# Moving 25 small weight strips out of a state scan, and a gate product made of seven smaller ones

## The reference, cut to what matters

```python
sh_a, sc_a, g_a, sh_f, sc_f, g_f = split(silu_c @ w_mod + b_mod, 6)      # "modulation", 6 x 1024 columns
hx = x * (1 + sc_a) + sh_a                                               # the first two sixths are needed early
proj = hx @ w_in                                                         # z, q, xbc, dt, k, v
y = ssd_scan(forward) + ssd_scan(backward) + xs * d_skip                 # chunked state scan, 8 chunks of 128 tokens
y = y * silu(z);  y = y * rsqrt(mean(y*y over each half)) * ssd_norm_g   # the gate, z = hx @ w_in[:, 0:1024]
q, k = rope(rms_norm(q)), rope(rms_norm(k))
o = softmax(q @ [k_ctx, k].T) @ [v_ctx, v]
x = layer_norm(alpha * x + g_a * ([y, o] @ w_out))                       # g_a and later ones: the second modulation
```

## Time and profile before

| | us |
|---|---|
| median of 3 runs | 3060.01 |
| profiled execution, its own time | 3059.18 |
| span of its trace | 3057.1 |
| PE busy in the span | 2879.1 (94%) |
| DVE, ACT, POOL busy | 1593.1, 749.8, 1078.1 |
| granted TensorE clock, mean | 0.969 |

### The profile page before, as it was taken

One profiled execution on the slowest core, in us unless ns is written; L12 is line 12 of the kernel. 1 busy time (PEld: TensorE's weight loads), 2 busy tenths in 40 slices (PEclk: granted clock), 3 DMA queues, 4 the chain that ended last, 5 costly groups with the idle time before them and its releaser, 6 DMA issues. The chain is left out here.

```text
span 3057.1 us, 28739 instructions
## 1 busy us (share of the span) xinstructions
PE 2879.1 (94%) x10163; PEld 1404.6 (46%) x10163; DVE 1593.1 (52%) x2480; ACT 749.8 (25%) x1573; POOL 1078.1 (35%) x971
## 2 busy tenths in 40 slices
PE   7998999999899999999869994988999999999999
PEld 4554554444444444344534442565444444444443
DVE  2434884345767777556654435455644444444446
ACT  2223755511133333400311115222030000000002
POOL 0001881000177777700022004831024555555442
PEclk9999999999899999999879996999999999999999
DMA  7001332100100000020368987003020111111101
GB/s 279 21 0 31 95 103 73 55 28 1 56 1 1 1 1 1 1 70 24 89 249 347 375 318 239 4 14 111 1 83 28 42 55 62 49 42 42 42 14 62
DMA packets 130686, 237.51 MB, mean 78 GB/s; under 512 B 25544, under 2 KB 81520, under 8 KB 120688
## 3 DMA queue, kind: packets, MB, share of 16 engines
q1 hardware_dynamic: 120016, 206.11, 19.0%
q0 software_dynamic: 5760, 16.78, 1.8%
q10 hardware_dynamic: 4768, 12.79, 1.1%
HBM read 235.65 MB, written 26.22 MB: 86 GB/s over the span
## 5 line engine op out<-in xcount | busy, mean ns | idle before, releaser
L3614 DVE TENSOR_TENSOR arena_d<-arena_d,ps 128x512 f32<-128x512 f32 x154 | 102.0, 686 | 387.6 <-PE ps L3489 387.6
L3454 POOL TENSOR_TENSOR arena_b<-arena_b,arena_d 128x512 f32<-128x512 f32 x120 | 150.9, 1271 | 362.6 <-DVE arena_d L3636 361.3
L1383 DVE TENSOR_REDUCE arena_b<-ps 128x1 f32<-128x512 f32 (+1 forms) x384 | 212.0, 597 | 122.8 <-PE ps L1263 119.9
L1365 POOL TENSOR_TENSOR arena_b<-arena_b 128x512 f32<-128x512 f32 x182 | 224.8, 1272 | 70.8 <-ACT arena_b L1346 70.8
L3633 DVE TENSOR_TENSOR arena_b<-arena_b,ps 128x512 f32<-128x512 f32 x240 | 158.9, 685 | 32.5 <-POOL arena_b L3454 23.7
L1263 PE MATMUL ps<-arena_d,arena_a 64*128 64x512 f32 (+1 forms) x768 | 169.7, 529 | 3.0 <-DVE arena_b L1374 2.9
L1281 PE MATMUL ps<-arena_a,arena_d 64*128 64x512 f32 x640 | 169.3, 600 | 0.0
L1077 PE MATMUL ps<-ring,arena_b 128*128 128x512 f32 x384 | 167.4, 592 | 0.0
L564 PE MATMUL ps<-arena_b,ring 128*128 128x512 f32 x384 | 167.1, 593 | 0.0
L3489 PE MATMUL ps<-arena_a,ring 128*128 128x512 f32 x352 | 154.4, 597 | 3.2 <-DMA ring<-in_w_up 3.2
L1346 ACT ACTIVATE arena_b<-ps 128x512 f32<-128x512 f32 x214 | 116.0, 595 | 135.8 <-PE ps L1287 135.8
(11 more groups left out here) (615 smaller groups left out, 5432.8 us busy)
## 6 DMA issues: line engine op xcount, KB each, us to landing
ring<-in_w_gate SPq DMA_DIRECT2D x33, 1024.0 KB
ring<-in_w_up SPq DMA_DIRECT2D x33, 1024.0 KB
ring<-in_w_down SPq DMA_DIRECT2D x33, 1024.0 KB
ring<-in_w_in SPq DMA_DIRECT2D x10, 2048.0 KB, 9.5
ring<-in_w_mod SPq DMA_DIRECT2D x32, 512.0 KB, 3.8
yslots<-arena_a ACTq DMA_DIRECT2D x24, 512.0 KB
arena_d<-in_w_gate SPq DMA_DIRECT2D x10, 1024.0 KB
arena_d<-in_w_up SPq DMA_DIRECT2D x10, 1024.0 KB
```

The source lines that it names most:

```text
L1365: eng.tensor_tensor(acc, first, prT[n % NPR], ALU.add).then_inc(s_pa, 1)
L1383: eng.tensor_reduce(mx3[j % 2][:, t, e, piece:piece + 1], ps[:, shared("s", u), 0:k1 - k0], AX.X, ALU.max).then_inc(s_mx, 1)
L3454: eng.tensor_tensor(o, o, dsum[0 if a == "a12" else 1], ALU.add).then_inc(s_comb, 1)
```

## The change

What it does:
- Only the strips 0 to 6 stay around the scan. Strips 7 to 31 move: 13 stand on PE between the transposes of job 16 and those of job 17, 6 between the first twelve score pairs of attention, 3 between the next ones and 3 in attention's first job. They have four buffers in ring slot 0, a bank of their own, and DMAs that are issued once the key products are done.
- The gate product becomes seven half-depth products per pair of token tiles (Winograd's scheme on 2x2 blocks): 28 products of four 128x512 matmuls. GpSimd makes the sums of inputs and one sum of weights, DVE three sums of weights (128x2048) and the additions between products.
- GpSimd sets up attention's constants instead of DVE.
- The reload of `hc`, the loads of the q panels and of the w_out panels move later on SP's queue.

```diff
-        NSTRIP = 32
+        NSTRIP, EARLY = 32, 7
...
-        def strips_by(k):
-
-            return EARLY + min(NSTRIP - EARLY, (NSTRIP - EARLY) * (k + 1) // 24)
+        BEFORE_TURN, IN_JOB = 13, 3
+        S_TURN = EARLY + BEFORE_TURN
+        S_JOB = NSTRIP - IN_JOB
...
+            if i == EARLY:
+                eng.wait_ge(s_rawz, MOD_SET[2] + 2)
+                eng.wait_ge(s_qkTc, NJ - 2)
...
+        def pe_next_strip(eng, i):
+            if i != EARLY:
+                pe_strip_sum(eng, i - 1)
+            pe_strip(eng, i)
...
         def sp_gate(eng):
             after(eng, "ssd")
             load_panels(eng, J_Z + 1, J_KV)
-            eng.dma_start(hc.rearrange("p k n -> p (k n)"), hc_dram).then_inc(s_spill, 16)
...
-            load_panels(eng, J_KV, NPAN1)
+            load_panels(eng, J_KV, J_Q)
+            eng.wait_ge(s_z, NZP)
+            eng.dma_start(hc.rearrange("p k n -> p (k n)"), hc_dram).then_inc(s_spill, 16)
+            load_panels(eng, J_Q, J_OUT)
+            eng.wait_ge(s_qkp, NT)
+            for i in range(EARLY, NSTRIP):
+                b = (i - EARLY) % 4
+                if i >= EARLY + 4:
+                    eng.wait_ge(s_mod, 4 + i - 3)
+                eng.dma_start(strip2[b], strip_of(i)).then_inc(s_xl[b], 16)
+            eng.wait_ge(s_mod, 4 + NSTRIP)
+            load_panels(eng, J_OUT, NPAN1)
+
+        def pool_z_sums(eng):
+            after(eng, "ssd")
+            for g in range(NG):
+                z1, z2, z3, z4 = zsum[g % 2]
+                if g >= 2:
+                    eng.wait_ge(s_z, zmade("p3", g - 2))
+                eng.tensor_tensor(z1, hx_part(1, 0, g), hx_part(1, 1, g), ALU.add).then_inc(s_zi, 1)
+                eng.wait_ge(s_zi, zsummed("z1", g))
+                eng.tensor_tensor(z2, z1, hx_part(0, 0, g), ALU.subtract).then_inc(s_zi, 1)
+                eng.tensor_tensor(z3, hx_part(0, 0, g), hx_part(1, 0, g), ALU.subtract).then_inc(s_zi, 1)
+                eng.wait_ge(s_zi, zsummed("z2", g))
+                eng.tensor_tensor(z4, hx_part(0, 1, g), z2, ALU.subtract).then_inc(s_zi, 1)
+                if g == 1:
+                    wait_panel(eng, J_Z)
+                    eng.wait_ge(s_zw, ZW0 + 2)
+                    eng.tensor_tensor(zt4, z21, zt2, ALU.subtract).then_inc(s_zi, 1)
...
 # dve_gate, new order: three weight sums, then the units
+            weight_sum(1, zt1, z12, z11)
+            weight_sum(2, zt2, z22, zt1)
+            weight_sum(3, zt3, z22, z12)
+            for u, (c, g) in enumerate(ZUNITS):
+                t, n = ztile(c, g)
+                if c == "c22" and g >= 1:
+                    first_adds(g)
+                if u >= 1:
+                    normed(u - 1)
+                adds(u)
                 v = y[:, t, n * HALF:(n + 1) * HALF]
...
 # act_qkv, behind job 17's Square and Sqrt and the copy of job 16's transposes
+                if j == NJ - 1:
+                    for i in range(EARLY, S_TURN):
+                        act_strip(eng, i)
...
         def pool_att(eng):
+            eng.wait_ge(s_qkp, NJ)
+            eng.tensor_copy(identb, ident[:, :]).then_inc(s_mc, 1)
+            for v in (oneb[:, 0:64], oneb[:, 64:128]):
+                eng.memset(v, 1.0).then_inc(s_mc, 1)
+            for v in mcat:
+                eng.memset(v, 0.0).then_inc(s_mc, 1)
+            eng.memset(rec, 1.0).then_inc(s_mc, 1)
             after(eng, "qkv")
```

More of the change, by code:

```diff
@@ new lines, in pe_gate @@
+            TURNS = {("p5", 0): ("c11", 0), ("p4", 0): ("c11", 1)}
+            for g in range(1, NG):
+                TURNS[("p6", g)] = ("c22", 0) if g == 1 else ("c11", g)
+                TURNS[("p7" if g == 3 else "p1", min(g + 1, 3))] = ("c21", g - 1)
+                TURNS[("p5", g)] = ("c12", g - 1)
+                if g < 3:
+                    TURNS[("p3", g)] = ("c22", g)
+            for name, g in ZORDER:
+                product(name, g)
+                if (name, g) in TURNS:
+                    turn(zunit(*TURNS[(name, g)]))
@@ L994, in pe_gate, with copied @@
             pe_qkv_product(eng, 0)
-            turn(2 * LT - 1)
+            for u in range(2 * LT - 3, 2 * LT):
+                turn(u)
+            pe_qkv_product(eng, 1)
         def act_gate(eng):
             after(eng, "ssd")
-            for u, (n, t) in enumerate(ZUNITS):
-                eng.wait_ge(s_z, u + 1)
-                if u >= 4:
-                    eng.wait_ge(s_zg, u - 3)
-                eng.activation(zs[u % 4], ps[:, u % 4, :], ACT.Silu).then_inc(s_zs, 1)
+            def copied(g):
+                eng.wait_ge(s_z, zmade("p1", g))
+                if g >= 2:
+                    eng.wait_ge(s_za, zadded("c12", g - 2))
+                eng.copy(zu2[g % 2], zbank("p1", g)).then_inc(s_zc, 1)
@@ new lines, in act_gate @@
+            copied(0)
+            copied(1)
+            for u, (c, g) in enumerate(ZUNITS):
+                t, n = ztile(c, g)
+                if c == "c11":
+                    eng.wait_ge(s_z, zmade("p2", g))
+                    if u >= 4:
+                        eng.wait_ge(s_zg, u - 3)
+                    eng.activation(zs[u % 4], zbank("p2", g), ACT.Silu).then_inc(s_zs, 1)
+                else:
+                    eng.wait_ge(s_za, zadded(c, g))
+                    eng.activation(zs[u % 4], zs[u % 4], ACT.Silu).then_inc(s_zs, 1)
+                if c == "c12" and g + 2 < NG:
+                    copied(g + 2)
@@ L1292, in pv @@
                 n = 20 * j + 2 * kt
+                if kt == 0 and j == 0:
+                    eng.wait_ge(s_modc, 5)
                 if kt == 0 and j >= 1:
@@ L1306, in row_sums @@
                 mm.then_inc(s_sum, 1)
+            strips = iter(range(S_TURN, NSTRIP))
             for pair in range(12):
                 scores(0, pair)
+                if pair % 2:
+                    pe_next_strip(eng, next(strips))
             for pair in range(3):
@@ L1312, in pe_att @@
             turn_shifts(0)
+            pe_next_strip(eng, next(strips))
             for pair in range(3, 6):
                 scores(1, pair)
+                if pair < 5:
+                    pe_next_strip(eng, next(strips))
             for j in range(NJOB):
@@ L1317, in pe_att @@
                     shifted(j, kt)
+                    if j == 0 and kt < IN_JOB:
+                        pe_next_strip(eng, next(strips))
+                    if j == 0 and kt == IN_JOB:
+                        pe_strip_sum(eng, NSTRIP - 1)
                     for ahead, pair in BESIDE[kt]:
```

281 lines of the change are left out of this document (206 added, 75 removed).

## The result

The changed kernel takes 3091.0 us (median of 4 runs, 3089.07 to 3092.99), the kernel before 3060.3 beside it (3059.5 to 3061.07): a ratio of 1.0101, interval 1.0089 to 1.0113. It is slower by 1%, some five times what a measurement can tell from no change. The forecast was 3068, range 3053 to 3075. The direction was right, the size was not. The profiled execution (3089.07, span 3087.3) is 30.2 us longer in span than that of before.

What follows compares the result with a forecast made beforehand. The scan was taken as bound by PE and nearly as hard by DVE and GpSimd taking turns. Terms -4.0 - 7.8 + 14.5 + 1.1 + 4.9 = +8.7 us gave 3067.9 for the profiled execution; forecast 3068, range 3053 to 3075.

Steps and rivals of the forecast that it cites:

- Term 1: Scan: taking the strips out saves PE time, -4.0 us, bounds +3 and -12.
- I take 0.3 per chunk: Scan: each of five steady chunks falls by the 0.29 us idle piece of DVE and GpSimd, 1.5 us in all.
- the count of the two engines' turns: Scan: DVE and GpSimd instructions that can't overlap sum to 21.1 to 22.9 us per chunk, against 22.13 measured.
- The upper bound of +3: Scan: slowest case, turns fall worse at 22.9 us a chunk, less the 2.5 of the other two items.
- Term 2: Gate: 16 matmuls fewer give -13.8 us, waits and late work return 6.0; -7.8, bounds -12.5 and -4.
- Term 3: Thirteen strips ahead of job 17's transposes: mostly low-clock turns of 1.79 us; +14.5 us, bounds +10 and +17.
- Rival A: Clock holds through the strips, DMA sets their end at 811.9; 3064 us in all, chance 0.24.
- Term 4: Attention's constants on GpSimd come behind its tables and delay the first scores; +1.1 us, bounds +0.5 and +2.
- Term 5: Twelve strips in attention: 0.8 us each on PE, partly hidden; +4.9 us, bounds +2.4 and +8.
- About five of the six hide: Attention's first twelve pairs: DVE sets the pace, so about five of six strips cost nothing; low-clock opening adds, +1.3 us.
- B: Scan is PE's after all: six chunks near 20.5 us save 12, not 4; 3053.8 us, chance 0.15.
- C: Strips' chain slower still, late DMA plus low clock, 2.1 us a turn instead of 1.79; 3072 us, chance 0.13.

Runs made afterwards that it cites:

- experiment 1: Changed kernel plus 128x128 matmuls on constants (eight or four) ahead of the scan's diagonal products that wait anyway; 3079.5 us.
- experiment 3: Changed kernel with one of GpSimd's two decay terms per quad of the scan left out (decays not the reference's); 3073.8 us.
- experiment 8: Changed kernel with the 25 strips back in the scan and attention's constants back on DVE, leaving the seven-product gate and later loads; 3056.5 us, ratio 0.9988 to the kernel before.
- traces of 1 to 7: One execution each of seven variants of the changed kernel, all with the same gate; 3073.8 to 3091.8 us.
- experiment 9: experiment 8 plus one wait: GpSimd starts its 128x2048 weight sum only after DVE's first gating product; 3049.1 us, ratio 0.9967 to the kernel before.
- Experiment 6: Changed kernel plus 128x128 products on constants behind the thirteen strips' products ahead of job 17's transposes, eight behind the first, one behind each other; 3088.3 us.
- Experiment 7: Changed kernel without its last twelve strips, those in attention (their modulation columns aren't computed); 3084.1 us.

## Why the prediction was wrong

**Term 1, the scan, is the step that failed**, by 12.2 of the 19 us in the sum. "I take 0.3 per chunk" rested on the count of the two engines' turns, and this count was good: at the high clock a chunk came to 21.98 us against 21.1 to 22.9. Left out was what the idle PE does to its clock. Five steady chunks make 7.7 of the 8.5 us. The working named the 1.74 us wait at 468.70 as proof that PE gets ahead, and did not go on to the rows of PE behind it, still in the trace of before:

```profile
469.75 2.02 PE L871 MATMUL ps<-ring,m_gt 128*128 128x512 f32 x2
471.56 1.70 PE L872 MATMUL ps<-ring,m_lt 128*128 128x512 f32 x2
```

Elsewhere these take 1.08 and 1.02. Every chunk without strips was to have such a wait. With the carried product late, the cost fell on the two engines that set the pace. The upper bound of +3 was for worse turns; it had no such case, and by its own figures (0.8 us in each of five chunks, less 2.5) it would have been +1.4. With the waits filled the scan takes 163.5 us where before it took 167.8: -4.3, against the -4.0 of the sum (experiment 1). So what the term lacked was the clock, some 12 us, and nothing else of that size; its parts fit less well (a chunk fell by 0.15 us, not 0.3). Weighing the Trainium skill's rule (SBUF — State Buffer, "Who interferes with whom") against the rows was right as far as it went (experiment 3 confirms that GpSimd's share counts), but it is a rule for VectorE and GpSimd and says nothing of PE's clock.

**Term 2, the gate, held**: -7.9 against -7.8, one wait of 3.34 us where 3 to 4 was said, no later ones over 1 us. That the number fits so well is luck in part. The hold-up of DVE's product by GpSimd's sum was there as described, but GpSimd's sum takes 4.51 us, not the 3.8 worked out from half its size, and it ran into DVE's third sum as well, which made it 6.55. Against that PE came into the gate slow (16 matmuls in 15.99 us, 14.00 in experiment 8), so less of the delay was left to wait for, and the 1.5 us of later waits in the sum never came. The same gate gave only 5.0 in experiment 8 (5.2 to 8.1 in the traces of 1 to 7), and 11.0 with the hold-up removed (experiment 9), inside the bounds.

**Term 3, the thirteen strips, had the right mechanism and was 3 us short.** The turn at the low clock was put at 1.79 us, from 1.35 and the 0.44 of the strip's products. The sum's products slow down too, 0.38 to 0.59, and it was 1.98, from the second strip on rather than the fourth. 0.19 x 9 and two turns of 0.63 are 3.0 us, which is what is missing. Rival A (the clock holds) is refuted for the chain as it stands. Experiment 6 held the clock in part and gained 2.2 us where A gave 3.2 for this stretch: its second limit, the transfers, is there, and lies higher than it said.

**Term 4, the constants:** +1.6 for +1.1, at the release named.

**Term 5, attention:** +8.4 for +4.9, a little outside the bound of 8. "About five of the six hide" was wrong. A strip with its sum moves the next scores by 829.53 - 828.49 = 1.04 us, and by 0.88 at a sum's 0.38; twelve are some 10.7 us, and 8.4 of them are seen. Of the other 2.3, 1.1 are the waits that before had there; what hid the rest isn't shown. DVE's 18 maxima in 9.26 us ran without a pause, but PE was busy 15.64 us for 30 scores as well: that one engine never stands still did not show that the other one has time. Experiment 7 removes 6.6 of the 8.4.

**The rivals.** B (PE sets the scan's pace) was excluded: with the clock held a chunk is 21.98. C had the direction right, for half its reason: the strips' turn was slower than 1.79, by the clock alone, and no transfer was late. None of the rivals comes near 3091, since the forecast and all three let the scan save time.

## What to carry to other kernels

Before taking work off PE in a stage that it shares with other engines, look at what PE does behind its longest wait there: if matmuls behind such a wait are slower in the trace, work removed is a wait grown, and it can cost more than it frees. If it must go, fill the wait or check that what follows it isn't on the pace-setting chain. A chain that PE shares in small pieces with ACT, like the strips here, is to be priced whole at the low clock, the small products in it too. Where two engines hold each other up, the long instruction of the one with time to spare is best started after the short one of its neighbour that others wait for.

## What the runs showed of the hardware

- In the scan a wait of 1.36 us left the next 128x512 float32 matmul at 1.08 us, one of 2.16 us was followed by matmuls of 1.79 and 1.91; in the gate a wait of 4.31 us was followed by 6.58 us for four, one of 3.34 us by 3.67. Longer waits are not always followed by slow work: what stood ahead of the wait differed too, and what decides was not isolated.
- A strip's products, 32 columns wide, and its sum, 1.98 us a turn, ran at a granted clock of 0.50, 1.2 GHz of 2.4, for over 20 us; with one 128x128 product more in each turn (experiment 6) the same chain ran at 1.00 up to its fourth wait for a transfer, near 810 us, and at 0.50 from 811 on.
- A 128x2048 subtraction with two SBUF inputs took 4.51 us on GpSimd. Started 0.11 us behind a DVE sum of that size (2.29 us) it took 6.55, and the DVE product of two SBUF inputs that came next took 4.88 in place of 0.69. The Trainium skill (SBUF — State Buffer, "Who interferes with whom") says that a VectorE instruction with two SBUF inputs contends with a GpSimd one that reads SBUF, and calls the shared ports an exclusive lock. The rows agree: each took longer by about what the earlier one still had to run (2.0 of 2.2 us, 4.2 of 4.3).
- In experiment 9 a DVE scaling with one SBUF tensor as its input (L1219), started 2.3 us into GpSimd's sum, took 2.46 us in place of 0.49. No product of PE waited for it.
